# Differential attention step: one maximum instruction for both components, and the output squares taken per token tile in the next stage

## The chip, the cores and the metric

The kernel runs on one core of one Trainium2 chip. The metric is the device time of one execution in microseconds (us). The kernel before takes 1469.76 us (median of 3 runs, 1469.55 to 1470.68).

## The reference, cut to what matters

One decoder layer: an input projection; Mamba-2 and differential attention side by side; an output projection; cross-attention into 256 memory tokens; a squared-ReLU MLP. The change touches the differential attention and what follows it:

```python
def block(i):                                   # 128 queries, 4 heads, 2 components
    s = einsum('bhcqd,bhckd->bhcqk', qb, k) * scale
    s = where(causal, s, -inf)
    p = softmax(s, axis=-1)
    attn = p[:, :, 0] - lam * p[:, :, 1]
    return einsum('bhqk,bhkv->bhqv', attn, v)
o = rms_norm(o, subln_w) * (1.0 - lambda_init)  # over the 128 values of each head
```

The sequence has 1024 tokens in 8 tiles of 128. Everything is float32.

## The kernel before, in words

**The attention steps.** A step is one token tile `i` (128 queries) and one head `h`; there are 32. `ATT_STEPS` orders them in pairs of a long tile and a short one: tiles 7 and 3 for the four heads (steps 0 to 7), then tiles 6 and 2 (8 to 15), 5 and 1 (16 to 23), 4 and 0 (24 to 31). A step of tile `i` has `(i + 1) * 128` keys. The scores of a long step lie in PSUM banks 0 to 3 (two banks for each component), those of a short step in banks 4 and 5 (one for each).

Each engine has its own loop over `n`, in a fixed order written out by hand, and semaphores join them:

- TensorE: the scores of step `n` (they wait until both exponentials of step `n - 2` are done), closed by one mask matmul for each component (L2357), which signals `s_done`; then the transposes of the first four blocks of step `n - 2` (L2372), the product with the values of step `n - 3` (L2391), and the transposes of the other blocks of step `n - 2`, which use the same bank as the first four.
- VectorE: the negated maximum of component 0 of step `n` (L1643), the combination of step `n - 1` (reciprocal L1652, ratio L1653, and L1655 over all keys), the maximum of component 1 of step `n` (L1643 again).
- ScalarE: the copy of the transposed probabilities of step `n - 2` out of PSUM (L1020), the copy of the output of step `n - 3` (L1035) and its square with a sum over the 128 values (L1040), the second copy of probabilities, and the two exponentials of step `n` with their sums (L1003).

The exponential of a component waits for the maximum of that component. The transposes of a step wait for its combination.

**Extra work within the stage.** ScalarE squares the two memory tiles in its iterations 6 and 7 (L843); VectorE normalises them in iteration 9 (L1390). For each token tile, six iterations after its last head is combined or later, VectorE takes the mean of the output squares (L1374), GpSimd the power (L770), and VectorE scales the four heads (L1665).

**The end of the stage.** TensorE transposes the memory tiles in iterations 32 and 33 (L2211), ScalarE and VectorE split them in two parts each (L849, L1383), and TensorE starts the memory projections when both are split.

**The memory projection stage.** 16 steps of products with 256 columns for the memory keys and values. After every second step TensorE transposes one token tile of the mixer's output, in the order `MIX_TILES`; ScalarE evacuates each step (L1061), splits the weights (L838), and copies the transposed tile; VectorE makes the low parts.

## Time and profile before

| | |
|---|---|
| median of 3 runs | 1469.76 us |
| profiled execution, its own time | 1469.96 us |
| its span, first to last instruction | 1468.2 us |
| mean granted TensorE clock | 0.996 |
| TensorE matmul busy | 1434.4 us (98%) |
| VectorE busy | 942.7 us (64%) |
| ScalarE busy | 674.8 us (46%) |
| GpSimd busy | 89.0 us (6%) |

PE is TensorE's matmul unit and PEld its weight loads, DVE is VectorE, ACT ScalarE, POOL GpSimd. A row of the timeline gives the start and the duration in us; in square brackets stands how long the engine had been idle and what released it. "x8" means that eight records in a row are merged, and a float32 matmul of the scores and of the values product leaves two records.

### The profile page before, as it was taken

How to read it: one execution, taken by the hardware profiler on the slowest of the kernel's cores; microseconds unless marked ns; L12 is line 12 of the kernel's file. 1: busy time of each engine (PE TensorE's matmuls, PEld its weight loads, DVE VectorE, ACT ScalarE, POOL GpSimd, SP SyncE). 2: the span in 40 equal slices, each digit the busy share in tenths (PEclk: the TensorE clock that was granted, in tenths of full speed). 3: DMA queues.
4: the chain of work that ended last, by engine and by line, in shares of the span. 5: the costliest groups of instructions: out<-in, count | busy, mean ns of one | idle time of the engine just before them, and what ended most of it. 6: DMA issues, size and time to landing. Idle time of an engine off the chain costs nothing.

```text
span 1468.2 us, 19715 instructions
## 1 busy us (share of the span) xinstructions
PE 1434.4 (98%) x7272; PEld 1191.3 (81%) x7280; DVE 942.7 (64%) x1519; ACT 674.8 (46%) x1370; POOL 89.0 (6%) x132
## 2 busy tenths in 40 slices
PE   9999999998989999999999999999999999999998
PEld 8889888885669988888787877888888788888886
DVE  4883565628885434543553789887776585467897
ACT  6324222328885423432532565444454464444443
POOL 1000000000010001010000360000000000000011
PEclk9999999999999999999999999999999999999999
DMA  9212011102003612311221343664343697765463
GB/s 318 60 30 58 29 30 29 58 1 87 1 1 116 232 65 77 115 58 43 72 101 58 121 130 115 215 197 172 148 158 117 240 352 258 260 227 188 157 229 129
DMA packets 94606, 185.52 MB, mean 126 GB/s; under 512 B 10160, under 2 KB 28592, under 8 KB 92464
## 3 DMA queue, kind: packets, MB, share of 16 engines
q1 hardware_dynamic: 87312, 153.30, 30.8%
q10 hardware_dynamic: 7200, 30.97, 6.2%
q8 instruction: 58, 0.95, 0.3%
q14 instruction: 36, 0.29, 0.1%
HBM read 142.30 MB, written 41.94 MB: 125 GB/s over the span
## 4 chain that ended last, share of the span: by engine, by line
PE 87%; DVE 4%; ACT 4%; issue 3%; DMA 1%; SPq 1%; ACTq 0%; DVEq 0%; POOLq 0%; POOL 0%
PE ps L2152 26%; PE ps L2154 26%; PE ps L2153 26%; PE ps L2211 1%; ACT probs L1003 1%; DVE nmax L1643 1%; PE ps L2294 1%; DMA x_in<-in_x_dram 1%; PE ps L2391 1%; PE ps L2353 1%; PE ps L2372 1%; PE ps L2297 1%; ACT junk L843 0%; PE ps L2512 0%; PE ps L2312 0%
## 5 line engine op out<-in xcount | busy, mean ns | idle before, releaser
L2152 PE MATMUL ps<-wh,oph 128*128 128x512 f32 (+1 forms) x576 | 216.0, 375 | 0.0
L2154 PE MATMUL ps<-wh,opl 128*128 128x512 f32 (+1 forms) x576 | 212.0, 368 | 0.0
L2153 PE MATMUL ps<-wl,oph 128*128 128x512 f32 (+1 forms) x576 | 211.9, 368 | 0.0
L2152 PE MATMUL ps<-d_ring 128*128 128x512 f32 x448 | 174.6, 390 | 2.1 <-DVE d_ring L2026 2.1
L2154 PE MATMUL ps<-d_ring 128*128 128x512 f32 x448 | 174.5, 390 | 0.0
L2153 PE MATMUL ps<-d_ring 128*128 128x512 f32 x448 | 174.3, 389 | 0.0
L770 POOL TENSOR_TENSOR rms<-stat,mhalf 128x1 f32<-128x1 f32 (+2 forms) x59 | 52.6, 893 | 1329.3 <-DVE stat L1374 1307.6
L2154 PEld LDWEIGHTS ps<-wh,opl 128*128 128x128 f32 x576 | 108.3, 188 | 19.2
L2152 PEld LDWEIGHTS ps<-wh,oph 128*128 128x128 f32 x576 | 108.3, 188 | 17.8 <-ACT vt L963 0.2
L2153 PEld LDWEIGHTS ps<-wl,oph 128*128 128x128 f32 x576 | 108.4, 188 | 17.6
L1292 ACT ACTIVATE d_ring<-left_raw 128x512 fp32r<-128x512 f32 x112 | 70.3, 628 | 98.0 <-PE ps L2154 77.3
L2020 DVE TENSOR_TENSOR d_ring<-left_raw,d_ring 128x512 fp32r<-128x512 f32 x112 | 78.2, 699 | 54.8 <-ACT d_ring L1292 54.5
L2152 PE MATMUL ps<-oph,wq_h 128*128 128x512 f32 x256 | 100.8, 394 | 3.9 <-DVE wq_l L1898 2.0
L2152 PE MATMUL ps<-oph,wh 128*128 128x512 f32 x256 | 101.1, 395 | 0.7 <-DVE wl L1370 0.4
L2152 PEld LDWEIGHTS ps<-d_ring 128*128 128x128 f32 x448 | 84.1, 188 | 20.4 <-issue 2.5
L2154 PE MATMUL ps<-oph,wq_l 128*128 128x512 f32 x256 | 100.6, 393 | 0.0
L2153 PE MATMUL ps<-opl,wq_h 128*128 128x512 f32 x256 | 100.5, 393 | 0.0
L2154 PE MATMUL ps<-oph,wl 128*128 128x512 f32 x256 | 100.4, 392 | 0.0
L2153 PE MATMUL ps<-opl,wh 128*128 128x512 f32 x256 | 100.3, 392 | 0.0
L2153 PEld LDWEIGHTS ps<-d_ring 128*128 128x128 f32 x448 | 84.2, 188 | 17.4
L2154 PEld LDWEIGHTS ps<-d_ring 128*128 128x128 f32 x448 | 84.1, 188 | 17.5
L1370 DVE TENSOR_TENSOR wl<-raw,wh 128x1024 fp32r<-128x1024 f32 (+1 forms) x44 | 53.4, 1224 | 33.5 <-ACT wh L838 32.8
(358 smaller groups left out, 2938.0 us busy)
## 6 DMA issues: line engine op xcount, KB each, us to landing
right_raw<-in_w_down_dram SPq DMA_DIRECT2D x128, 256.0 KB, 3.9
u_kept_s<-us SPq DMA_DIRECT2D x64, 256.0 KB, 2.3
left_raw<-u_kept_s SPq DMA_DIRECT2D x64, 256.0 KB, 2.8
w_blk<-in_w_up_blocks_dram ACTq DMA_DIRECT2D x14, 1024.0 KB, 6.0
left_raw<-u_kept_a SPq DMA_DIRECT2D x48, 256.0 KB, 3.2
raw<-in_w_in_dram SPq DMA_DIRECT2D x16, 512.0 KB, 3.9
u_kept_a<-u SPq DMA_DIRECT2D x24, 256.0 KB, 2.3
x_in<-in_x_dram SPq DMA_DIRECT2D x8, 512.0 KB, 9.3
```

The source lines that it names most:

```text
L770: g.tensor_tensor(dst, src, mhalf[:, 0:w], ALU.pow).then_inc(rms_ready, 1)
L1003: s.activation(probs[:, n % 2, c, 0:keys], src[:, 0:keys], ACT.Exp, bias=nmax[:, n % 2, c:c + 1], accum_out=sums[:, n % 4, c:c + 1]).then_ ...
L1292: s.activation(d_ring[m % DRING][:, 0, :], left_raw[:, m % 4, :], ACT.Copy).then_inc(dn_hi, 1)
L1370: v.tensor_tensor(wl[:, slot, part], raw[:, q % 2, n], wh[:, slot, part].bitcast(F32), ALU.subtract).then_inc(w_lo, 1)
L1643: v.tensor_reduce(nmax[:, n % 2, c:c + 1], src[:, 0:keys], AX.X, ALU.max, negate=True).then_inc(mx_done[c], 1)
L2020: v.tensor_tensor(ring[:, 1, :], left_raw[:, m % 4, :], ring[:, 0, :].bitcast(F32), ALU.subtract).then_inc(dn_lo, 1)
L2152: te.matmul(o, lh, rh, start=first, stop=False)
L2153: te.matmul(o, lh, rl, start=False, stop=False)
L2154: return te.matmul(o, ll, rh, start=False, stop=last)
L2211: ins = te.transpose(ps[:, tr_bank(n) + b, k * P:(k + 1) * P], src(4 * b + k), ident[:])
L2294: te.matmul(ps[:, 4, h * 64:(h + 1) * 64], cb_decay[:, h, :], xdt[:, h * 64:(h + 1) * 64], start=True, stop=True)
L2297: ins = te.matmul(ps[:, 6, gr * 256:(gr + 1) * 256], b_cb[:, gr, :], xdt_end[:, gr * 256:(gr + 1) * 256], start=True, stop=True)
```

## The change

`s_done` and `mx_done` become one semaphore each. One `tensor_reduce` reads both components of a step and writes both maxima; it waits for both mask matmuls and stands ahead of the combination of step `n - 1`. The square with its sum is taken out of the step. In its place `o_square` squares the four heads of one token tile at a time from SBUF, and VectorE adds them up (`tensor_reduce`) ahead of the mean. Tiles 0 and 1 of `MIX_TILES` are squared in ScalarE's iterations 32 and 33 of the attention loop; tiles 2 to 7 in steps 2, 4, ... 12 of the memory projection stage. Their means are taken in the same steps and the scaling one step later.

```diff
+O_SQUARE_AT = {2 * m - 2: m for m in range(2, NT)}
+O_NORM_AT = {2 * m - 1: m for m in range(2, NT)}
...
+        o_part = [at(f"o_part{n}", "TMP", 9216 + 2048 * n, [P, DH, P]) for n in range(2)]
...
@@ ScalarE
             def attn_exp(n, c):
-                act.wait_ge(mx_done[c], n + 1)
+                act.wait_ge(mx_done, n + 1)
...
+            def o_square(m):
+                i = MIX_TILES[m]
+                act.wait_ge(o_ev, O_STEP[i] + 1)
+                if m >= 2:
+                    act.wait_ge(ms_ready, POW[("o", MIX_TILES[m - 2])] + 1)
+                else:
+                    act.wait_ge(sq_done, 2 * NT)
+                s.activation(o_part[m % 2][:], mix[:, 4:8, i * P:(i + 1) * P], ACT.Square).then_inc(o_sq, 1)
...
             for n in range(NS + 3):
+                if n in (NS, NS + 1):
+                    o_square(n - NS)
                 if n >= 3:
-                    s.activation(mix[:, 4 + h, i * P:(i + 1) * P], o, ACT.Copy, scale=recs[:, k % 4, 0:1])
-                    if k >= 4:
-                        act.wait_ge(o_ev, k - 3)
-                    elif k == 0:
-                        act.wait_ge(sq_done, 2 * NT)
-                    s.activation(junk[:, (k % 4) * P:(k % 4 + 1) * P], o, ACT.Square, scale=recs[:, k % 4, 0:1],
-                                 accum_out=stat[:, COL[("o", i)] + h:COL[("o", i)] + h + 1]).then_inc(o_ev, 1)
+                    s.activation(mix[:, 4 + h, i * P:(i + 1) * P], ps[:, 7, 0:P], ACT.Copy,
+                                 scale=recs[:, k % 4, 0:1]).then_inc(o_ev, 1)
...
             for n in range(16):
+                if n in O_SQUARE_AT:
+                    o_square(O_SQUARE_AT[n])
@@ VectorE
-            def attn_max(n, c):
-                keys = (steps[n][0] + 1) * P
-                dve.wait_ge(s_done[c], n + 1)
+            def attn_max(n):
+                i = steps[n][0]
+                dve.wait_ge(s_done, 2 * n + 2)
                 if n >= 2:
-                    dve.wait_ge(ex_done[c], n - 1)
-                b = score_bank(steps[n][0], c)
-                src = ps[:, b:b + 2, :].rearrange("p b k -> p (b k)")
-                v.tensor_reduce(nmax[:, n % 2, c:c + 1], src[:, 0:keys], AX.X, ALU.max, negate=True).then_inc(mx_done[c], 1)
+                    dve.wait_ge(ex_done[0], n - 1)
+                    dve.wait_ge(ex_done[1], n - 1)
+                b, nb = score_bank(i, 0), 2 if i >= 4 else 1
+                src = ps[:, b:b + 2 * nb, :].rearrange("p (c b) k -> p c (b k)", c=2)
+                v.tensor_reduce(nmax[:, n % 2, :], src[:, :, 0:(i + 1) * P], AX.X, ALU.max, negate=True).then_inc(mx_done, 1)
...
-            def o_mean(i):
-                dve.wait_ge(o_ev, O_STEP[i] + 1)
+            def o_mean(m):
+                i = MIX_TILES[m]
+                dve.wait_ge(o_sq, m + 1)
+                after(v.tensor_reduce(stat[:, COL[("o", i)]:COL[("o", i)] + DH], o_part[m % 2][:], AX.X, ALU.add))
                 mean(("o", i), P, DH)
...
-            for n in range(NS + 7):
+            for n in range(NS + 3):
                 if n < NS:
-                    attn_max(n, 0)
+                    attn_max(n)
                 if 1 <= n <= NS:
                     attn_comb(n - 1)
-                if n < NS:
-                    attn_max(n, 1)
...
-                if n - 7 in O_COMPLETE:
-                    o_norm(O_COMPLETE[n - 7])
-                if n - 6 in O_COMPLETE:
-                    o_mean(O_COMPLETE[n - 6])
+                if n == NS + 1:
+                    o_mean(0)
+            o_mean(1)
+            o_norm(0)
+            o_norm(1)
 
             for n in range(16):
                 for q in split_at(name, st):
                     split_lo(q)
+                if n in O_NORM_AT:
+                    o_norm(O_NORM_AT[n])
+                if n in O_SQUARE_AT:
+                    o_mean(O_SQUARE_AT[n])
@@ TensorE, scores
-                    te.matmul(..., start=False, stop=True).then_inc(s_done[c], 1)
+                    te.matmul(..., start=False, stop=True).then_inc(s_done, 1)
```

## Rows read from the trace of the kernel before

**Rows 1.** Windows: stretch, length, busy of PE, PEld, DVE, ACT, POOL, clock, DMA.

```profile
333.00:450.00 117.00, 105.26 (x746) 76.08 (x747) 93.19 (x191) 97.44 (x286) 10.96 (x14) 0.99 0.07 24
448.00:504.00 56.00, 55.87 (x461) 55.05 (x460) 31.58 (x37) 30.75 (x50) 1.30 (x2) 1.00 0.51 155
354.62:362.12 7.50, 7.50 (x54) 5.18 (x53) 6.27 (x10) 6.67 (x17) 0.00 (x0) 1.00 0.00 0
...
404.65:410.41 5.76, 5.43 (x41) 3.90 (x41) 4.76 (x12) 5.18 (x18) 1.01 (x1) 1.00 0.00 0
427.32:432.44 5.12, 4.49 (x35) 3.39 (x35) 3.94 (x12) 4.56 (x19) 1.01 (x1) 1.00 0.01 3
```

**Rows 2.** Waits from 333 to 450: us in total, times, longest.

```profile
ACT probs L1003 <- DVE nmax L1643: 10.4, 20, 1.8
```

**Rows 3.** Timeline of PE in one pair of tiles 7 and 3.

```profile
356.54 0.29 PE L2357 MATMUL ps<-mask_q,ident_b 128*128 128x128 bf16 x2
...
359.79 0.61 PE L2372 MATMUL ps<-ident,probs 128*128 128x128 f32 x4
```

**Rows 4.** Timeline of DVE in the same pair.

```profile
356.81 1.23 DVE L1643 TENSOR_REDUCE nmax<-ps 128x1 f32<-128x1024 f32 x1 [0.30 <-PE ps L2357]
357.95 0.15 DVE L1652 RECIPROCAL recs<-sums 128x2 f32<-128x2 f32 x1
...
358.40 0.75 DVE L1655 SCALAR_TENSOR_TENSOR probs<-probs,ratio 128x512 f32<-128x512 f32 x1
```

**Rows 5.** Groups by form from 333 to 450: busy us, mean ns.

```profile
L1643 DVE TENSOR_REDUCE nmax<-ps 128x1 f32<-128x1024 f32 x8 | 9.7, 1219 | 1.5 <-PE ps L2357 1.5
...
L1643 DVE TENSOR_REDUCE nmax<-ps 128x1 f32<-128x128 f32 x8 | 2.3, 282 | 0.0
...
L1655 DVE SCALAR_TENSOR_TENSOR probs<-probs,ratio 128x128 f32<-128x128 f32 x4 | 1.4, 352 | 0.1
```

**Rows 6.** The tile of the later cross-attention's maxima: ns shortest/median/longest.

```profile
L1769 DVE TENSOR_REDUCE mmax<-ps x8: 1214/1218/1225, 685.0 to 749.1; 128x4 f32<-128x1024 f32 x8
```

**Rows 7.** Timeline of PE: masks and short step's transposes, tiles 5 and 1, 4 and 0.

```profile
406.14 0.28 PE L2357 MATMUL ps<-mask_q,ident_b 128*128 128x128 bf16 x2
...
408.75 0.39 PE L2372 MATMUL ps<-ident,probs 128*128 128x128 f32 x2
...
428.60 0.28 PE L2357 MATMUL ps<-mask_q,ident_b 128*128 128x128 bf16 x2
...
430.88 0.30 PE L2372 MATMUL ps<-ident,probs 128*128 128x128 f32 x1
```

**Rows 8.** Timeline of ACT: an output square, an exponential's end, a late exponential.

```profile
355.00 0.36 ACT L1040 ACTIVATE junk<-ps,recs 128x128 f32<-128x128 f32 x1
...
355.34 0.69 ACT L1003 ACTIVATE probs<-ps,nmax 128x512 f32<-128x512 f32 x1
...
432.06 0.23 ACT L1003 ACTIVATION_READ_ACCUMULATOR probs<-ps,nmax 128x1 f32 x1
...
439.36 0.37 ACT L1003 ACTIVATE probs<-ps,nmax 128x128 f32<-128x128 f32 x1 [0.54 <-DVE nmax L1643]
```

**Rows 9.** Timeline: TensorE's two disturbed waits within the stage, and the memory tiles' normalisation.

```profile
366.74 0.63 PE L2372 MATMUL ps<-ident,probs 128*128 128x128 f32 x4 [1.29 <-ACT probs_t L1020]
...
376.57 0.55 PE L2372 MATMUL ps<-ident,probs 128*128 128x128 f32 x3 [1.18 <-DVE probs L1655]
...
372.06 2.48 DVE L1390 SCALAR_TENSOR_TENSOR h_mem<-m_in,rms,gain_b 128x1024 f32<-128x1024 f32 x2
```

**Rows 10.** Timeline of PE at the end of the stage.

```profile
439.18 0.66 PE L2372 MATMUL ps<-ident,probs 128*128 128x128 f32 x4 [1.63 <-DVE probs L1655]
...
440.85 1.91 PE L2211 MATMUL ps<-ident,h_mem 128*128 128x128 f32 x8
...
444.40 1.04 PE L2211 MATMUL ps<-ident,h_mem 128*128 128x128 f32 x8
```

**Rows 11.** Window of the slow clock there.

```profile
441.00:442.00 1.00, 1.00 (x7) 1.00 (x6) 0.00 (x0) 0.35 (x2) 0.00 (x0) 0.50 0.00 0
```

More of the change, by code:

```diff
@@ L435, in build @@
         gate_done, lam_s = sem("gate_done"), sem("lam_s")
-        s_done = [sem(f"s_done{c}") for c in range(2)]
-        mx_done = [sem(f"mx_done{c}") for c in range(2)]
+        s_done, mx_done = sem("s_done"), sem("mx_done")
         ex_done = [sem(f"ex_done{c}") for c in range(2)]
         comb_done, pt_done, pt_ev, pv_done, o_ev = (sem(n) for n in ("comb_done", "pt_done", "pt_ev", "pv_done", "o_ev"))
+        o_sq = sem("o_sq")
         resid_loaded = sem("resid_loaded")
@@ L1033, in _ @@
                     act.wait_ge(pv_done, k + 1)
-                    o = ps[:, 7, 0:P]
-                    s.activation(mix[:, 4 + h, i * P:(i + 1) * P], o, ACT.Copy, scale=recs[:, k % 4, 0:1])
-                    if k >= 4:
-                        act.wait_ge(o_ev, k - 3)
-                    elif k == 0:
-                        act.wait_ge(sq_done, 2 * NT)
-                    s.activation(junk[:, (k % 4) * P:(k % 4 + 1) * P], o, ACT.Square, scale=recs[:, k % 4, 0:1],
-                                 accum_out=stat[:, COL[("o", i)] + h:COL[("o", i)] + h + 1]).then_inc(o_ev, 1)
+                    s.activation(mix[:, 4 + h, i * P:(i + 1) * P], ps[:, 7, 0:P], ACT.Copy,
+                                 scale=recs[:, k % 4, 0:1]).then_inc(o_ev, 1)
                 if n >= 2 and n - 2 < NS and steps[n - 2][0] >= 4:
@@ L1656, in attn_comb, with o_norm @@
                                        probs[:, n % 2, 0, 0:keys], ALU.mult, ALU.add).then_inc(comb_done, 1)
-            def o_mean(i):
-                dve.wait_ge(o_ev, O_STEP[i] + 1)
+            def o_mean(m):
+                i = MIX_TILES[m]
+                dve.wait_ge(o_sq, m + 1)
+                after(v.tensor_reduce(stat[:, COL[("o", i)]:COL[("o", i)] + DH], o_part[m % 2][:], AX.X, ALU.add))
                 mean(("o", i), P, DH)
-            def o_norm(i):
+            def o_norm(m):
+                i = MIX_TILES[m]
                 dve.wait_ge(rms_ready, POW[("o", i)] + 1)
@@ L2356, in scores @@
                     kn = (i + 1) * P - (i // 4) * 512
-                    te.matmul(ps[:, score_bank(i, c) + i // 4, kn - P:kn], ident_b[:], mask_q[:], start=False, stop=True).then_inc(s_done[c], 1)
+                    te.matmul(ps[:, score_bank(i, c) + i // 4, kn - P:kn], ident_b[:], mask_q[:], start=False, stop=True).then_inc(s_done, 1)
             def mem_tile(i):
```

## The prediction, made before the changed kernel was run

> **What bounds the kernel now.** The page comes first: TensorE is busy for 98% of the span, so a change counts only where TensorE waits. The windows by stage show where that is. In the memory projections (448 to 504) TensorE is busy for 55.87 of 56.00 us, while ScalarE and VectorE have 25 and 24 us free [rows 1]. In the attention stage (333 to 450) three engines are nearly level: TensorE 105.3, ScalarE 97.4, VectorE 93.2 of 117 us [rows 1]. The pair windows split it: a pair of tiles 7 and 3 takes 7.50 us with TensorE full; a pair of 5 and 1 takes 5.76 with 5.43 busy; a pair of 4 and 0 takes 5.12 with 4.49 busy [rows 1]. The wait list then offers a bait: ScalarE waits 10.4 us for maxima, 20 times [rows 2]. But ScalarE is not full in any pair, so the question is what TensorE waits for, and this is read off the timelines. VectorE's order decides it: maximum of component 0 of the long step, combination of the short step before it, maximum of component 1 [rows 4]. TensorE takes the short step's transposes at 359.79 without a gap; the combination ended at 358.40 + 0.75 = 359.15, 0.6 us ahead [rows 3, 4].
>
> **One maximum instruction, and its place.** First the price. One component costs 282 ns for 128 keys and 1219 ns for 1024 [rows 5], so 148 ns + 134 ns per 128 keys. The cross-attention's maximum over four rows of 256 costs 1218 ns, the same as one row of 1024 [rows 6], so rows are free and 2 x (i + 1) blocks cost 0.148 + 0.268 (i + 1): 2.29, 2.02, 1.76 and 1.49 us for tiles 7, 6, 5, 4. The next instruction starts 0.09 us before the display's end (356.81 + 1.23 against 357.95) [rows 4], so a merged step saves only 0.148 - 0.09, some 0.06 us of VectorE; over 32 steps 2 us, off the path. The bounds for the saving are 0 and 0.148 a step.
>
> Then the place. The combination of the short step now stands behind both maxima of the long one. From the long step's masks to the short step's transposes TensorE has other work for 359.79 - 356.54 = 3.25 us (tiles 7, 3), 2.61 us (5, 1), 2.28 us (4, 0) [rows 3, 7]; 6 and 2 lie between, 2.93. VectorE needs from the first mask: 0.27 until the maximum starts (356.81 - 356.54), 0.05 more because the second mask counts now (two masks in 0.12 us of TensorE, my estimate), the merged maximum less 0.08, 0.45 for reciprocal and ratio (357.95 to 358.40), the combination (0.75 for 512 keys, 0.35 for 128, so 0.62 and 0.48 between) and 0.03 to wake TensorE [rows 4, 5]. Sums: 3.75, 3.35, 2.95 and 2.55. So the transposes come late by 0.50, 0.42, 0.34 and 0.27 us in each pair. TensorE is in order, and the value product of the long step and the next scores stand behind them. Late once per pair, the delay adds up, because the next maximum starts only from the next masks. In short tiles part of it was idle anyway: the next scores waited for the second exponential, whose sum ended at 432.29, 0.15 before they began at 432.44 [rows 1, 8]. That hides 0.20 in a pair of 4 and 0 and about 0.1 in the two before.
>
> **Walk through the stage**, lateness of TensorE against the trace:
> - Start: the combination of step 1 falls behind the long maximum of step 2, but ScalarE's second exponential of step 1 comes earlier. Net +0.2.
> - Steps 4 to 7 (two pairs of 7 and 3): 2 x 0.50, now +1.2.
> - Steps 6 to 9: before, TensorE stood 1.29 us for a copy by ScalarE, which was behind the two memory squares [rows 9]. There ScalarE's queue counts: it is late by 0.6 as the merged maximum releases its exponential, and gains 0.34 from the output square left out (355.00 to 355.34) [rows 8]. TensorE's lateness is absorbed in its wait: +0.3.
> - Step 10: the normalisation holds VectorE for 2.4 us [rows 9]; the combination of step 9 now stands behind it and both maxima, so its transposes come 0.7 late, of which the next scores feel 0.5: +0.5. Then two pairs of 6 and 2 at about 0.3: +1.0.
> - Tiles 5 and 1: the first pair still combines 384 keys and had waited for the transposed copy, 0; then +0.2, +0.3, and -0.1 where two of VectorE's scalings (0.6 each) are gone: +1.5.
> - Tiles 4 and 0: 0.55 - 0.27 - 0.20 = about 0.1 a pair at most: +1.6.
> - End: an exponential waited 0.54 for its maximum behind the combination [rows 8], and TensorE 1.63 for the last long combination [rows 10]. In the new order the last short maximum is out early, and two scalings and two squares are gone from the way: -0.35 for the order, -0.25 for ScalarE's squares. +1.0 at the first memory projection.
>
> **The squares.** In a step they cost ScalarE 0.34 us [rows 8], 32 times, 10.9 us. TensorE waited for ScalarE's queue only at the memory squares and at the end, which is counted above; elsewhere the exponential is released by masks, maximum and copies. In their place stand eight squares of 512 values. No row shows one; four old ones bound it at 1.44 us, one old one from below at 0.34. I take 0.6 (the 128x512 exponential is 0.69) [rows 8]. Six of them in the memory projections are 3.6 us, at most 8.6, against 25 free. VectorE gets six sums and six scalings; each is under the 1.22 us of a 1024-wide instruction [rows 5], together under 15 against 24 free [rows 1]. The chain square, sum, mean, power, scaling has one step of the stage to run in (3.3 us a step, from 16 steps and the transposes in 56 us) and the transposes want it a step later, so I cost it at nothing. If the cover failed, TensorE would wait for a scaled tile, at most about 1 us each, six times. The two squares in iterations 32 and 33 lie where ScalarE waits for TensorE's memory transposes, now that the short squares are out.
>
> **A rule against the change.** VectorE is busy for 6.27 of 7.50 us in a pair of 7 and 3 [rows 1]: not saturated. The Trainium skill (Perfetto Trace Analysis, Optimizing Scalar/DVE Operations) says that grouping into larger operations improves throughput if the engine is saturated, and that where it is not, but causes bubbles elsewhere, breaking instructions up lets work complete sooner. It puts the fixed cost of a PSUM operand on VectorE at about 125 ns: by the first half this change would give back 32 x 0.125 = 4.0 us at most, by the second half it loses. The intercept of 148 ns agrees with the figure roughly, and the idle 1.2 us say that the second half applies.
>
> **Sum.** 1469.96 (the profiled execution's own time, 1.8 above its span) + 1.0 = 1471.0; the median was 0.2 lower than that execution, so 1470.8 us.
>
> **Rivals.**
> - *Waits removed, nothing put in their place.* If the short combination still arrives in time (a cheaper merged maximum, or slack that I read too small), the gains stand alone: 0.35 at the start, 0.35 at the memory squares, 0.3 at the normalisation, 0.4 for the scalings between 410 and 417, 0.3 of waits for exponentials, 0.6 at the end: 2.3, so 1467.5; and 1466.5 if the slow clock at the end also goes. For it: the 10.4 us of waits and two engines relieved. Against it: 3.75 against 3.25 us, from measured rows.
> - *The slow clock spreads* (the other side). At 441 to 442 the clock was at 0.50, the 1.2 GHz level, after TensorE had stood for 1.63 us and a little more; eight transposes took 1.91 instead of 1.04 us [rows 10, 11], with the work after them about 1.3 us in all. It did not fall after the waits of 1.29 and 1.18 [rows 9]. The wait of step 9's transposes grows from 1.18 to about 1.65, and each pair gets a new stall of 0.3 to 0.5. It decides if any of these tips the clock: one fall gives 1472.1, two 1473.4. Against it: within pairs the new stalls are short.
> - *The late squares bite.* If the scaled tiles come late in the memory projections, up to 1 us on each of six tiles: 1472 to 1476. Against it: the 24 free us.
> - *The merge does not do what it says.* Two rows in two banks each might cost as two instructions; then +0.06 a pair more, 1471.6. It belongs to the forecast.
>
> **Chances.** Forecast 0.62, waits removed 0.20, slow clock 0.12, late squares 0.06. What a measurement of this kernel can tell from no change is about 0.2%, 2.9 us: 1466.8 to 1472.7. Of the waits-removed case under half is below that, which with a little for the unforeseen gives 0.11 for faster; slower takes most of the last two cases: 0.13; within 0.2%: 0.76. The range leaves out the tails of the rivals: 1467.4 to 1473.2 us.
>
> **What would show it.** In the profile after: 32 maxima of about 2.3 us for tile 7 and under 0.45 us for tile 0; in a pair of 7 and 3 a new wait of TensorE's short transposes for the combination (L1655 before), about 0.5 us, and a period of 8.0 instead of 7.5; ScalarE's wait for maxima of short steps gone; first memory projection about 1 us later; the stage after it unchanged in length. A period of 7.5 would prove the central step wrong, and a stage shorter by more than 1 us the whole forecast.

## The result, and the profile after

The changed kernel takes 1473.96 us (median of 21 runs, 1472.93 to 1475.95 but for one of 1590.73 at a mean granted clock of 0.85, which the ratio leaves out) against 1470.42 us (21 runs, 1468.07 to 1471.45) beside it: ratio 1.0027, interval 1.0021 to 1.0032. It is 3.5 us slower; the forecast was 1470.8 us, no change. The profiled execution took 1473.2 us, its span is 1471.5 us against 1468.2.

The forecast's central step is there. The timeline of TensorE in a pair of tiles 7 and 3, then that of VectorE (start, us busy, engine, line, operation; in brackets the idle time before it and what ended it):

```profile
356.12 1.99 PE L2371 MATMUL ps<-kt,qt 64*128 64x512 f32 x8
358.04 0.28 PE L2375 MATMUL ps<-mask_q,ident_b 128*128 128x128 bf16 x2
...
361.83 0.66 PE L2390 MATMUL ps<-ident,probs 128*128 128x128 f32 x4 [0.37 <-DVE probs L1667]
362.32 1.95 PE L2409 MATMUL ps<-vt,probs_t 128*128 128x128 f32 x16
364.20 0.70 PE L2371 MATMUL ps<-kt,qt 64*128 64x512 f32 x2
```

```profile
358.36 2.29 DVE L1655 TENSOR_REDUCE nmax<-ps 128x2 f32<-128x2048 f32 x1 [1.61 <-PE ps L2375]
360.57 0.16 DVE L1664 RECIPROCAL recs<-sums 128x2 f32<-128x2 f32 x1
360.76 0.22 DVE L1665 SCALAR_TENSOR_TENSOR ratio<-sums,recs,lam 128x1 f32<-128x1 f32 x1
361.02 0.75 DVE L1667 SCALAR_TENSOR_TENSOR probs<-probs,ratio 128x512 f32<-128x512 f32 x1
```

Before, the combination ended 0.6 us ahead of the short step's transposes [rows 3, 4]; now these wait 0.37 us for it. The pair takes 8.08 us instead of 7.50: the wait, and 0.21 us more in which TensorE is shown as busy (7.71 against 7.50; the ends of matmuls are modelled in this profile). The windows (busy time of each engine, then granted clock, DMA share, GB/s), of the memory projections and of three pairs, answer to [rows 1]:

```profile
449.00:505.00 56.00, 55.62 (x459) 54.99 (x460) 40.14 (x56) 34.25 (x56) 10.48 (x7) 1.00 0.48 148
356.12:364.20 8.08, 7.71 (x54) 5.21 (x53) 6.15 (x9) 6.66 (x15) 0.00 (x0) 1.00 0.01 2
407.22:413.39 6.17, 5.62 (x41) 3.88 (x40) 4.53 (x9) 4.56 (x13) 0.00 (x0) 1.00 0.00 0
430.52:435.77 5.25, 4.56 (x35) 3.27 (x34) 3.78 (x8) 3.92 (x13) 0.00 (x0) 1.00 0.02 5
```

What was a wait of ScalarE has become one of TensorE. The waits from 333 to 453 us (us in total, times, longest): ScalarE's 10.4 us for maxima [rows 2] are 1.7, and TensorE's for the combination were 2.8 us in 2 waits (second fence, first line) and are 5.4 us in 12.

```profile
ACT probs L1006 <- DVE nmax L1655: 1.7, 2, 1.0
```

```profile
PE ps L2372 <- DVE probs L1655: 2.8, 2, 1.6
...
PE ps L2390 <- DVE probs L1667: 5.4, 12, 1.5
PE ps L2390 <- ACT probs_t L1023: 4.0, 9, 0.8
```

At the end of the stage two rows answer to [rows 10]: the wait is 1.11 instead of 1.63 us, and the eight memory transposes take 1.05 instead of 1.91 us, as the clock is at full speed. There was no slow clock here in this execution.

```profile
442.23 0.66 PE L2390 MATMUL ps<-ident,probs 128*128 128x128 f32 x4 [1.11 <-DVE probs L1667]
...
443.80 1.05 PE L2229 MATMUL ps<-ident,h_mem 128*128 128x128 f32 x8
...
449.04 0.36 PE L2170 MATMUL ps<-memh,wh 128*128 128x256 f32 x1 [1.41 <-ACT mix L1049]
```

**Where the 3.3 us of span are,** from landmarks of the two profiles: first memory projection 447.34 to 449.04, +1.70; the residual's first transposes 561.2 to 563.2, +0.3 more; the up projection's product 4 (it waits 2.05 us for wq_l in both) 849.62 to 851.59, the same +2.0; d_ring's wait of 2.08 us 1155.47 to 1158.72, +1.28 more; from there to the end nothing (312.7 and 312.8). So 1.28 us lie almost 400 us behind the last changed instruction, in identical code. TensorE's waits there, in before and then in the changed kernel (us in total, times, longest):

```profile
PE ps L2152 <- DVE wq_l L1898: 2.0, 1, 2.0
PE ps L2152 <- DVE u_s L1952: 1.8, 1, 1.8
```

```profile
PE ps L2170 <- DVE u_s L1970: 3.2, 1, 3.2
PE ps L2170 <- DVE wq_l L1916: 2.0, 1, 2.0
```

### The profile page after: what moved, and what is told of

Same layout as the page of the kernel before. It is cut to its first block, busy times and chain, and to the rows that moved or that the text cites. A ratio compares the mean times of both kernels' runs of the same rounds, so it can differ in the third digit from the quotient of the medians.

```text
span 1471.5 us, 19613 instructions
## 1 busy us (share of the span) xinstructions
PE 1436.3 (98%) x7272; PEld 1191.1 (81%) x7280; DVE 946.5 (64%) x1495; ACT 668.2 (45%) x1314; POOL 92.3 (6%) x132
## 4 chain that ended last, share of the span: by engine, by line
PE 88%; DVE 5%; ACT 3%; issue 3%; DMA 1%; POOL 0%; POOLq 0%; DVEq 0%; ACTq 0%
PE ps L2170 26%; PE ps L2172 26%; PE ps L2171 26%; PE ps L2371 2%; PE ps L2409 1%; DMA raw<-in_w_mv_dram 1%; PE ps L2312 1%; PE ps L2229 1%; DVE wl L1381 1%; PE ps L2390 1%; DVE wq_l L1916 1%; ACT probs L1006 1%; DVE probs L1667 1%; PE ps L2237 1%; PE ps L2315 0%
## 5 line engine op out<-in xcount | busy, mean ns | idle before, releaser
L773 POOL TENSOR_TENSOR rms<-stat,mhalf 128x1 f32<-128x1 f32 (+2 forms) x59 | 56.0, 952 | 1328.9 <-DVE stat L1385 1307.5
L1381 DVE TENSOR_TENSOR wl<-raw,wh 128x1024 fp32r<-128x1024 f32 (+1 forms) x44 | 53.5, 1224 | 28.0 <-ACT wh L841 27.8
```

The costliest lines, as they stand in the source:

```text
L773: g.tensor_tensor(dst, src, mhalf[:, 0:w], ALU.pow).then_inc(rms_ready, 1)
L1381: v.tensor_tensor(wl[:, slot, part], raw[:, q % 2, n], wh[:, slot, part].bitcast(F32), ALU.subtract).then_inc(w_lo, 1)
```

## The experiments

Fifteen runs, with their own runs of before beside each group. Medians are given with them; a span or a landmark is that of the profiled execution.

**Which part costs.** Two kernels do one part alone.

`squares_only`: the squares as in the change, the maxima in two instructions around the combination, as before.

```diff
-                    attn_max(n)
+                    attn_max(n, 0)
                 if 1 <= n <= NS:
                     attn_comb(n - 1)
+                if n < NS:
+                    attn_max(n, 1)
```

> The maxima as before (one per component, the combination of the step before between them); only the squares are moved. Theory P (the place of the maximum costs): the attention stage is shorter than before by about 1.5 us: 0.3 at the memory squares, 0.4 for the scalings that leave the stage, 0.6 to 1 at the end; first memory projection at about 445.8 instead of 447.3; the memory projections give back 0.3. Total 0.5 to 1.5 us faster than before, ratio 0.9995 to 0.999. Rival S (the moved squares are what costs, in the memory projections and after them): total 1.5 us or more slower than before.

Measured: 1470.21 us (before 1469.32), ratio 1.0005 [0.9996, 1.0014]: no difference, and the expected gain of 0.5 to 1.5 us is not there. First memory projection at 444.37, 3.0 us earlier than in before's first profile, the residual's transposes only 1.1 earlier: in this profile the clock fell behind that start, at 444.6 to 448.0, and not ahead of it as in before. Against the profile of before without a fall there (before_again, below) the start is 1.2 us earlier.

`max_only`: the kernel before with the merged maximum ahead of the combination.

> Only the merged maximum ahead of the combination; the squares stay in the steps. Theory P: a new wait of TensorE's short transposes for the combination in each pair of tiles 7 and 3, 6 and 2, 5 and 1, period 8.0 to 8.1 us for 7 and 3 instead of 7.5; the first exponential 0.7 us later; first memory projection 2 to 3.5 us later than before; total 2 to 4 us slower, ratio 1.0015 to 1.0027. Rival S: within 1 us of before.

Measured: 1473.66 us (before 1469.32), ratio 1.0027 [1.0018, 1.0036], all of the loss. First projection at 448.91.

**Is it the merging or the place?**

`two_ahead`: the changed kernel with a maximum instruction for each component, both ahead of the combination.

```diff
-                v.tensor_reduce(nmax[:, n % 2, :], src[:, :, 0:(i + 1) * P], AX.X, ALU.max, negate=True)
+                for c in range(2):
+                    v.tensor_reduce(nmax[:, n % 2, c:c + 1], src[:, c, 0:(i + 1) * P], AX.X, ALU.max, negate=True)
```

> As the changed kernel, but with two maximum instructions, both ahead of the combination. If the place costs and not the merging, the pairs of 7 and 3 take 8.1 to 8.2 us as in the changed kernel (8.07) or 0.07 more, the first exponential is back at its old time (0.7 earlier), total within 1 us of the changed kernel. If the merging itself cost (a wide read of four banks, one semaphore for two masks), this is faster than the changed kernel by 1.5 us or more.

Measured: 1473.31 us, ratio 1.0024 [1.0016, 1.0033]; a pair of 7 and 3 takes 8.08 us, its wait is 0.38. In the pairs it is the place: two instructions cost the same as one. At the start of the stage it is the merging: the first exponential again starts without a wait, at 336.51, where it waits until 337.53 in the changed kernel, and step 2's scores come 1.0 us earlier (0.7 by the time from step 0's). The first projection is at 448.17, 0.9 us ahead of the changed kernel's, but the residual's transposes are not (563.27 against 563.16), and the times can't be told apart.

`short_merged`: one merged instruction in short steps alone; in long steps the combination lies between the two maxima again.

> As the changed kernel, but the long steps keep one maximum ahead of the combination and one behind it; only the short steps have the merged maximum. Theory P: TensorE's short transposes find their combination done, 7.5 us a pair of 7 and 3, the start as before or 0.3 earlier, the end 0.6 or more earlier; first memory projection at 445 to 446; total 1 to 3 us faster than before, 4 to 6 us faster than the changed kernel. Rival S: at least 1 us slower than before.

Measured: 1468.18 us, ratio 0.9991 [0.9982, 1.0000], 5.5 us below max_only and 5.1 below two_ahead, which has its squares, both run beside it. Its timelines of VectorE and TensorE in a pair of 7 and 3:

```profile
356.15 1.23 DVE L1657 TENSOR_REDUCE nmax<-ps 128x1 f32<-128x1024 f32 x1 [0.95 <-PE ps L2379]
...
357.74 0.75 DVE L1669 SCALAR_TENSOR_TENSOR probs<-probs,ratio 128x512 f32<-128x512 f32 x1
```

```profile
355.88 0.29 PE L2379 MATMUL ps<-mask_q,ident_b 128*128 128x128 bf16 x2
...
359.13 0.61 PE L2394 MATMUL ps<-ident,probs 128*128 128x128 f32 x4
```

The combination starts at 357.74, 1.86 us behind the masks at 355.88, as in before (358.40 - 356.54 [rows 3, 4]); in the changed kernel it is 361.02 - 358.04 = 2.98. The transposes have no wait, and the period is 7.5.

`max_behind`: the combination first, the merged maximum behind it.

```diff
-                if n < NS:
-                    attn_max(n)
                 if 1 <= n <= NS:
                     attn_comb(n - 1)
+                if n < NS:
+                    attn_max(n)
```

> The changed kernel with VectorE's order turned round: combination of step n-1 first, then the merged maximum of step n. Theory (the place in VectorE's queue decides, because each waits for something that the other lets happen): now the maximum can't start before the second exponential of the step before, and the chain exponential, combination, maximum, exponential, combination, maximum has nothing beside it; a pair of tiles 7 and 3 takes about 10 us instead of 8.07, a pair of 4 and 0 about 6.7 instead of 5.25, together 25 to 30 us more: about 1500 us. Rival (what costs is only that the short combination stands behind the long maximum): with the combination ahead, the short transposes are never late, the period falls back to 7.5, and the kernel comes to 1468 to 1470 us.

Measured: 1501.69 us (2 runs), 27.2 above the changed kernel run beside it (1474.45). Pairs take 10.27 us (7 and 3) and 7.82 (4 and 0; 6.7 was expected). The rows of VectorE and TensorE show the chain without anything beside it: the maximum can't start before the combination (365.29), this not before ScalarE's sum.

```profile
364.84 0.17 DVE L1664 RECIPROCAL recs<-sums 128x2 f32<-128x2 f32 x1 [1.57 <-ACT probs L1006]
...
365.29 0.75 DVE L1667 SCALAR_TENSOR_TENSOR probs<-probs,ratio 128x512 f32<-128x512 f32 x1
365.96 2.29 DVE L1655 TENSOR_REDUCE nmax<-ps 128x2 f32<-128x2048 f32 x1
```

```profile
370.72 0.70 PE L2371 MATMUL ps<-kt,qt 64*128 64x512 f32 x2 [1.21 <-ACT probs L1006]
```

**Do the squares cost anything in the memory projections?** `squares_late`: short_merged with ScalarE's square behind the rounding of the step's weights.

```diff
-                if n in O_SQUARE_AT:
-                    o_square(O_SQUARE_AT[n])
                 for q in split_at(name, st):
                     split_hi(q)
+                if n in O_SQUARE_AT:
+                    o_square(O_SQUARE_AT[n])
```

> The kernel that merges the maximum in short steps only (1468.18 us, first memory projection at 442.94, first residual transposes at 558.0), with ScalarE's squares of the outputs in the memory projections moved behind the rounding of the weights of their step. There TensorE waits 0.53 and 0.41 us for VectorE's lower halves of the weights, after ScalarE's rounding had waited for weight transfers, which start only when both halves are made. Theory (the six squares cost something because they stand ahead of the weights in ScalarE's queue, 0.6 us each, which puts off the next transfer): the waits at 483 and 497 us fall below 0.2, the residual transposes come 0.5 to 1.0 us earlier, 1467.4 us. Rival (VectorE's sums and scalings, 0.7 us each, do it, or the transfers themselves are the limit): waits and time unchanged, within 0.3 us of 1468.2.

Measured: 1468.33 us (before 1470.32), ratio 0.9983 [0.9974, 0.9992]. The wait at 483 is gone, that at 497 stays (0.47), the residual's transposes start at 557.5, 0.5 earlier. The median equals that of short_merged, so the time tells nothing. The landmark doesn't decide it either: this stretch differs by up to 1.4 us between profiles whose code in it is the same (below, under the squares).

**What repeats?** The two kernels once more.

> The kernel before, unchanged, profiled once more. In its first profile TensorE waits 1.28 us at 713 us and 1.84 us at 882 us for VectorE's u_s; in the profiles of the four changed kernels so far there is no wait at 713 and one of 3.16 to 3.18 us at 882 (the changed kernel) or the same place. Theory A: the MLP part of the loss (about 1.3 us at 882) is a property of the change; then this profile shows 1.28 and 1.84 again within 0.1. Theory B: both belong to one execution and come and go (the transfers fall differently); then this profile may show another pair of values, and the 1.3 us must not be booked to the change. Time 1469 to 1470.5 under both.

> The changed kernel, unchanged, profiled once more. Theory A: wait of 3.2 us at 884 us again, first memory projection at 449.0, first residual transposes at 563.2. Theory B: the first two numbers that lie before 600 us repeat within 0.2 us, the wait at 884 us differs. Time 1473 to 1474 under both, ratio to before 1.0025.

Measured: 1470.22 (before beside it 1470.32) and 1474.45 us. The changed kernel repeats: 448.86, 563.3, a wait of 3.17 us at 884. Before does not: its first memory projection comes at 445.54 instead of 447.34, and the wait of 1.28 us at 713 is gone (here the clock fell ahead of it, at 704.6 to 708.0, and in the first profile it did not). The wait for u_s stays (1.73). Most of the 1.80 us at the first projection is in the granted clock (the other 0.28 us were there before the wait of 1.63). Before at 440 to 444 us (clock: third column from the right), first profile, then second:

```profile
440.00:442.00 2.00, 1.45 (x8) 1.42 (x8) 0.64 (x3) 1.35 (x5) 0.00 (x0) 0.61 0.00 0
442.00:444.00 2.00, 2.00 (x12) 2.00 (x11) 0.19 (x1) 0.99 (x3) 0.00 (x0) 0.54 0.00 0
```

```profile
440.00:442.00 2.00, 1.67 (x15) 1.70 (x16) 0.40 (x2) 1.29 (x7) 0.00 (x0) 1.00 0.00 0
442.00:444.00 2.00, 1.95 (x17) 1.68 (x15) 1.29 (x2) 2.00 (x7) 0.00 (x0) 1.00 0.00 0
```

The same kernel, the same wait of 1.63 us ahead: once it went on at 1.2 GHz for 3.4 us, which is 1.7 us of full-speed time (2.00 x (0.39 + 0.46)), and once at 2.4. From the end of that wait to the first projection it took 8.16 us (439.18 to 447.34) and 6.64 (438.90 to 445.54): the fall cost 1.5 us there. And behind the wait for wq_l the clock fell in both profiles of before, and in none of the changed kernel's, which falls at 884, behind the wait of 3.2 us. The windows of before (first profile), then of the changed kernel:

```profile
850.00:852.00 2.00, 2.00 (x6) 1.53 (x5) 1.90 (x4) 0.35 (x1) 0.36 (x1) 0.51 0.00 0
852.00:854.00 2.00, 2.00 (x7) 1.61 (x6) 2.00 (x5) 1.95 (x5) 2.00 (x2) 0.64 0.00 0
...
884.00:886.00 2.00, 2.00 (x11) 1.65 (x10) 2.00 (x4) 1.97 (x5) 1.32 (x1) 1.00 0.00 0
```

```profile
852.00:854.00 2.00, 2.00 (x11) 1.63 (x10) 1.90 (x4) 0.37 (x1) 0.38 (x1) 1.00 0.00 0
...
882.00:884.00 2.00, 0.00 (x0) 0.00 (x0) 2.00 (x5) 0.04 (x1) 0.00 (x0) 1.00 0.00 0
884.00:886.00 2.00, 1.93 (x6) 1.63 (x7) 2.00 (x4) 1.97 (x4) 0.00 (x0) 0.72 0.00 0
886.00:888.00 2.00, 2.00 (x6) 1.52 (x5) 1.53 (x3) 1.97 (x5) 1.62 (x1) 0.50 0.00 0
```

This gave a second theory: between 850 and 884 VectorE's chain sets the end (it is busy without a break at 882 to 884 while TensorE does nothing). By it a slow clock ahead of that wait is hidden in it, and one behind it costs in full. Seven kernels put idle transposes of the identity into TensorE's stream to move the falls.

```diff
+                        for _ in range(14):
+                            te.transpose(ps[:, bank, 0:P], ident[:], ident[:])
```

`before_fill` (ahead of the up projection's product 0) and `before_fill_up2` (ahead of product 2), each in the kernel before:

> The kernel before with fourteen idle transposes of the identity (about 1.8 us of TensorE, their output overwritten at once) put into TensorE's wait of 2.05 us for the first lower weights of the up projection (847.9 in before). In both profiles of before the granted clock fell to 0.50 right behind that wait, TensorE's ten products from there are about 1.7 us later, and it waits 1.73 to 1.84 us at 881 to 882 for VectorE's u_s; in all changed kernels the clock stayed at 1.00 there, the wait for u_s is 3.17 us, and the clock falls behind that. Theory (VectorE's chain sets the end of this stretch, so a slow clock ahead of it costs nothing and one behind it costs 1.4 us): with the clock held up at 850 the wait for u_s grows to 3.2, the clock falls behind it, d_ring's wait starts about 1.3 us later relative to the start of the up projection, and the kernel is about 1.3 us SLOWER than before (1471.6 against 1470.3). Rival (the slow clock at 850 costs what it takes, and the 1.3 us of the changed kernels come from something else): 1.7 us faster, or no change.

> The kernel before with fourteen idle transposes (1.7 us) in front of the up projection's product 2, the one that waits 2.05 us for its lower weights and behind which the clock fell in both profiles of before. (The transposes of the run before_fill stood two products earlier, at 832 us, where VectorE's chain starts, and only delayed it.) Theory: the wait shrinks to about 0.5, the clock stays at 1.00 behind it, TensorE therefore waits 3.17 instead of 1.73 us for u_s at 880, the clock falls there, and from the start of the up projection to d_ring's wait it takes 307.2 instead of 305.9 us; the kernel is 1.3 us slower than before, unless a later fall that before shows at 1154 goes. Rival (a slow stretch costs what it takes): 1.7 us faster.

Measured: 1471.59 (before 1470.09) and 1471.61 us (before 1470.25). Both were misplaced: the wait of 2.05 us is that of product 4. It did not shrink, and the transposes delayed everything behind them by some 1.5 us, since VectorE's chain starts from TensorE's. So neither time decides anything, though both hit the expected number. The second profile still helps: this time the clock did not fall behind the same 2.05 us, and then the wait for u_s was 3.17 us and the clock fell at 884, with the code of before. Its windows:

```profile
852.00:854.00 2.00, 1.81 (x8) 1.51 (x9) 1.90 (x4) 0.00 (x0) 0.00 (x0) 1.00 0.00 0
...
884.00:886.00 2.00, 1.34 (x3) 1.11 (x4) 2.00 (x4) 1.42 (x3) 0.00 (x0) 0.68 0.00 0
886.00:888.00 2.00, 2.00 (x6) 1.58 (x5) 2.00 (x4) 1.97 (x5) 1.04 (x1) 0.50 0.00 0
```

`after_fill_up` (the changed kernel, ahead of product 13):

> The changed kernel with the same fourteen idle transposes placed in front of the up projection's product 13, the one before the wait of 3.17 us for u_s. TensorE comes to that wait 1.8 us later, VectorE does nothing else than before. Theory: wait 1.4 us instead of 3.17, the product starts at the same time, the clock does not fall behind it, and the kernel is 1.4 us faster than the changed one (1472.6 against 1474.2). Rival (the clock falls whatever fills the wait, or TensorE's lateness is handed on to VectorE): same time, or up to 1.8 us slower.

Measured: the wait is 1.57 us, the clock does not fall there, and d_ring's wait ends 305.72 us after product 4's instead of 307.13. But the clock now fell from 1157.6, behind d_ring's wait (which ended at 1157.18), where it had not in the changed kernel, and the time is 1474.55 us (6 runs), no gain. The mechanism was right, the time wrong: a fall prevented at one place came at another. The rest of the kernel took 314.1 us instead of 312.8, which gives back the 1.4. It is so in the other executions too, by their mean granted clock: the one profile with two falls (late_fill_end, the fall in the last microseconds counted) has 0.998, those with three have 0.996 or 0.997, and all six executions of after_fill_up have 0.996 or 0.997, none 0.998.

`late_fill` (squares_late, in the wait for the first cross-attention probabilities) and `late_fill_both` (ahead of product 13 as well):

> The fastest kernel so far (short steps merged, squares behind the weights; 1468.3 us) with fourteen idle transposes in TensorE's wait of 2.10 us for the first cross-attention probabilities (701 us). In seven of eight profiles of kernels with that wait the clock fell to 0.50 behind it for about 3.3 us. Theory: wait 0.3, no fall, 1.6 us faster: 1466.7. Rival (the stretch behind is set by another engine, or the clock falls a little later anyway): within 0.4 us of 1468.3.

> The kernel before this one with the transposes in front of product 13 as well. Theory: the gains add, 1.6 + 1.4: 1465.3 us, and the clock is low in the last microseconds alone. Rival: as for the two before it, 1468.3.

Measured: 1468.07 and 1468.59 us (before 1470.09). The rival holds for the first: the clock stays up, but the next probabilities are then waited for 1.40 us, and from the residual's transposes to the last of these waits it takes as long as in squares_late (557.52 to 754.06, 196.5; here 559.24 to 755.94, 196.7). A fall ahead of a wait for another engine's chain cost nothing here. The gains do not add; in late_fill_both the wait for u_s is 1.56 us, and the clock fell from 1154.2, behind d_ring's wait, as in after_fill_up.

`before_fill_end` (before, with twelve transposes in the wait of 1.63 us at the end of attention) and `late_fill_end` (the same in squares_late):

```diff
-                pe.wait_ge(comb_done, k + 1)
                 if m:
                     pe.wait_ge(pt_ev, m)
+                if (k, part) == (NS - 2, 0):
+                    for _ in range(12):
+                        te.transpose(ps[:, 6, 0:P], ident[:], ident[:])
+                pe.wait_ge(comb_done, k + 1)
```

> The kernel before with twelve idle transposes (1.3 to 1.5 us) in TensorE's wait of 1.63 us for the last long combination of attention. Of two profiles of before the clock fell behind this wait in one (first memory projection 447.34) and not in the other (445.54). Theory (before runs in two modes because this fall comes in some executions; the changed kernel's wait there is 1.11 us and its clock never fell in six profiles): no fall, first memory projection at 445.6, and a median nearer to the lower mode, 1468.5 to 1469.5 against 1470.3. Rival (the two modes of before come from elsewhere): first projection at 445.6 as well, but the same median, within 0.4 us.

> The kernel with short steps merged and squares behind the weights (1468.3 us) with the same twelve transposes in its wait of 1.41 us at 436. Behind this wait the clock fell in two of four profiles of kernels with this attention part. Theory: no fall, first memory projection at 443.0, median 0.8 us lower: 1467.5. Rival: 1468.3 unchanged.

Measured: 1468.91 us, 1.3 below before (1470.25), ratio 0.9990 [0.9981, 0.9999], just clear of none, and a range of 1468.12 to 1469.85 where before spreads from 1467.76 to 1473.11. The wait is filled and the clock holds:

```profile
437.22 1.53 PE L2372 MATMUL ps<-ident 128*128 128x128 f32 x12 [0.25 <-ACT probs_t L1020]
438.59 0.60 PE L2375 MATMUL ps<-ident,probs 128*128 128x128 f32 x4
...
440.04 1.04 PE L2211 MATMUL ps<-ident,h_mem 128*128 128x128 f32 x8
...
445.10 0.36 PE L2152 MATMUL ps<-memh,wh 128*128 128x256 f32 x1 [1.42 <-ACT junk L1040]
```

late_fill_end takes 1467.21 us, 3.0 below before, ratio 0.9983 [0.9973, 0.9993]: of all kernels the lowest median, 6.75 us below the changed one.

**The seventeen profiles together.** From product 4 to d_ring's wait the time has two values. It is 305.75 to 305.90 us in the four where the clock fell behind product 4's wait (before, before_again, before_fill, late_fill_end; wait for u_s 1.73 to 1.84), and 305.69 and 305.72 in the two with transposes ahead of product 13. It is 307.05 to 307.13 us in the other eleven: no fall there, a wait of 3.16 to 3.18 us, and a fall behind it in each. Both values occur with the code of before (305.85; 307.05, 307.06 in before_fill_up2 and before_fill_end) and with changed code (305.90 in late_fill_end; 307.13). So before's code can lose the 1.28 us too. Whether the change makes it more frequent is open: before's code gave the longer value in two of five profiles, the changed kernel and the two with its maxima (max_only, two_ahead) in all four that have no transposes there. The fall right behind the last wait for the combination came in three of the four profiles of before's attention without a filled wait, in one of five of the kernels whose short steps or squares alone are changed (late_fill, from 437.8; in squares_only and late_fill_both one came later, from 444.6 and 444.2, behind the wait of 1.41 us at the start of the memory projections), and in none of the five with the long maxima ahead of the combination. In max_behind, where that wait is 2.60 us, it came too.

## Why the prediction was wrong

**The pairs: right.** Predicted lateness of the short transposes 0.50, 0.42, 0.34 and about 0.1 us (tiles 4 and 0, after what is hidden); the periods grew by 0.58 (7.50 to 8.08), 0.36 (6.77 to 7.13 in the second profiles), 0.42 (5.76 to 6.18) and 0.13 (5.12 to 5.25). The terms hold as well: from the masks to the transposes it is 361.83 - 358.04 = 3.79 us against the 3.75 of the sum. One of them, 0.03 us to wake TensorE, stands in no row that it names; the traces have 0.06 (361.02 + 0.75 to 361.83). The merged maxima take 2292, 2023, 1758 and 1492 ns, to 10 ns as computed. two_ahead and short_merged show that the place is the cause in the pairs.

**The walk through the stage: the step that failed.** It reached +1.6 us ahead of the end. Measured at the scores of each step: +0.67 at step 2, +2.08 at step 8, +1.05 at 9, +1.20 at 10, +2.13 at 16, +3.02 at 24, +3.35 at 30. The terms that were mis-sized:
- Start, +0.2 forecast, +0.67 measured. ScalarE's first exponential now waits until both long maxima are there, and nothing stood in front of it. Before it started at 336.85 without a wait, and in two_ahead too; so this term is the merging's own. Now:

```profile
337.53 1.11 ACT L1006 ACTIVATE probs<-ps,nmax 128x1024 f32<-128x1024 f32 x1 [0.71 <-DVE nmax L1655]
```

- Steps 2 to 8: I counted two pairs at 0.50; there are three, and they cost 0.27, 0.56 and 0.58. Together with the start this is +2.08, not the +1.2 of the walk.
- The memory squares: the absorption was right, 1.03 us against 0.9. From 8 to 10 the lateness falls to +1.20 (forecast +0.5).
- Tiles 6 and 2, three pairs: 0.14, 0.36, 0.43, where I booked two at about 0.3 (0.5 + 0.6 is 1.1; the walk has +1.0). Tiles 5 and 1: 0.09, 0.35, 0.42, 0.03, where I booked 0.2 and 0.3 with a gain of 0.1 for two scalings that VectorE no longer does. Neither that gain is seen, nor the tenth of a us per pair that I took off as hidden: the full prices were 0.42 and 0.34.
- Tiles 4 and 0: 0.3 against 0.1. The end: -0.30 against -0.6, from +3.35 to +3.05 (439.18 to 442.23).

At the end of attention this is +3.05 where the walk had +1.0. Of the 2.05 us between them about 0.8 are pairs that were not booked (0.41 + 0.14 + 0.23), 0.5 the hiding that did not come, 0.5 the start and 0.3 the end. The largest fault is the count: the mechanism was priced for a pair and then booked for too few. With my own prices, hiding and all, three pairs of each kind are 3 x (0.50 + 0.3 + 0.25 + 0.1) = 3.45 us; plus 0.2 for the start, less 0.9 and 0.6, that is +2.15, and +2.8 if only the pairs of 4 and 0 hide anything.

**The clock: not in the sum.** The sum went against a profile with a fall at 440 to 444 [rows 11] and kept its 1.3 us (1.5 by the second profile) as if they belonged to the kernel. Of four profiles of before's attention one has no fall; against it the changed kernel's first projection is 3.3 us late (445.54, 448.86), not 1.7. before_fill_end supports by the time that this fall is a cost which before pays in part of its executions: without it the median is 1.3 us lower. The changed kernel has it in none of its three profiles, and its wait there is shorter. So the account of the medians, argued from the profiles and not measured, is that the change loses about 3.3 us in the stage, gets back part of the 1.5, and loses up to 1.28 behind 884 where the clock does not happen to fall at 850. Measured in all: 3.5. That the loss is in the main not a matter of the clock can be seen without profiles: beside after_again, 13 of 27 executions of before had a mean granted clock of 0.997 and took 1470.1 us on average, and seven of the changed kernel's eleven had the same clock and took 1473.5.

**The slow clock as a rival: its place was wrong.** I priced more falls inside attention; in the changed kernel there is none. What differed is the wait at 884, 3.2 us instead of 1.8 with a fall behind it, that no row of mine covered, since I took everything behind the stage as shifted rigidly.

**The squares: nearly right.** Costed at nothing in the memory projections. From the first memory projection to the residual's transposes it takes 113.9 us in both profiles of before, and 114.1 to 114.5 in the changed kernel's three. But the four other profiles without the squares there take longer too: 114.3 in before_fill_end, 114.6 in max_only, 114.8 and 115.3 in before_fill_up2 and before_fill, with waits for weights of up to 0.9 us in all. The mean of all six is 114.5 us; that of the six with the squares ahead of the weights and no fall in the stretch (the changed kernel's three, two_ahead, short_merged, max_behind) is 114.6. A small cost can't be told from that spread. In attention the squares alone bring 1.2 us (squares_only, against the profile of before without the fall), and its time shows no gain. short_merged, which keeps the place of the long combination, starts the memory projections 2.6 us earlier by the same comparison (445.54, 442.94), where the rival *waits removed* counted 2.3. Its median is 1.1 us below before's beside it, with an interval that reaches 1.0000; squares_late, with the same attention, is 2.0 below, clear of noise. So the rival was right on what there was to gain and wrong that this order lets it through.

**The rule against the change** pointed the right way: VectorE was not saturated, and longer instructions made a bubble on TensorE. That the 148 ns of a start could be saved played no part: two_ahead, which pays it, is not slower than the change (1473.31, against 1473.66 of max_only beside it). The merging had a price of its own instead, once: the first exponential, 0.7 us.

**Open.** What decides whether the clock falls behind a given wait. Behind 3.2 us it fell eleven times of eleven, behind product 4's 2.05 us four times of seventeen, behind d_ring's 2.08 three of seventeen, and behind the 2.1 us for the first cross-attention probabilities thirteen of the fifteen times that it was not filled, with the same code ahead. So the length of the wait alone doesn't decide it. Open too is whether the change makes the longer way past 884 more frequent.

## What to carry to other kernels

An instruction merged out of two is worth its start-up time, and costs as much as its second half delays whatever stood between the two, and whoever could have started on the first half alone: before merging, look at who stood between, and at the slack of its consumer. Price such a delay per repetition and multiply by all repetitions; a walk that stops to absorb here and there loses count. Before summing against one profile, look for clock falls in it, and for each ask which engine's chain ends behind it: one hidden by a wait was free here, and it may vanish and reappear behind that wait in another kernel or another execution of the same one. The mean granted clock of the executions that were not profiled is a cheap second look.

## What the runs showed of the hardware

- In these seventeen profiles the granted clock falls to half in stretches of about 3.4 us. One cost 1.5 us at the end of attention (8.16 against 6.64), 1.4 behind d_ring's wait (314.1 against 312.8 to the end), and nothing ahead of a wait for another engine. Whether one comes differs between executions of one kernel: 1.63 us of idle TensorE at the end of attention was followed by it in the first profile of before and not in the second.
- VectorE's sums of 128x512 with both inputs in SBUF, 0.68 us elsewhere, take up to 1.8 us while GpSimd works on tiles of that size; those with one input in PSUM keep 0.68 us. In that profile 19 with both inputs in SBUF ran for the most part beside such a GpSimd instruction: 12 took 0.80 to 1.80 us, 7 kept 0.68. The 12 all began 0.2 to 1.1 us behind the start of a GpSimd instruction and ended 0.55 us behind its end; of the 7, six began with it or ahead of it. Of 17 with an input in PSUM none took more than 0.70. Ten of the 12 lie between 856 and 882, in VectorE's chain ahead of the wait at 884; what they add to that wait was not measured. From the second profile of the changed kernel, VectorE and GpSimd:

```profile
856.02 1.80 DVE L1916 TENSOR_TENSOR wq_l<-w_blk,wq_h 128x512 fp32r<-128x512 f32 x1
857.75 0.68 DVE L1970 TENSOR_TENSOR u_s<-ps,p_s 128x512 f32<-128x512 f32 x1
```

```profile
855.43 1.84 POOL L783 TENSOR_TENSOR t_sum<-raw_t,t_sum 128x512 f32<-128x512 f32 x1
```

The Trainium skill (SBUF — State Buffer, Who interferes with whom) says that a VectorE instruction with two SBUF inputs contends with a GpSimd instruction that reads SBUF, as they share a port, and one with at most one such input, outside the two-port modes, does not. The trace agrees, with 1.80 and 0.68 in the rows above; the seven of the 19 that kept 0.68 show that not every overlap costs.
- GpSimd's power of 4 columns takes 1.0 or 2.0 us in the memory projections, though nothing about its operands changes from one tile to the next. What changes is what VectorE had begun. In the eleven profiles with these powers, six in each behind the first, 19 began while VectorE's low part of the weights (L1381, both inputs in SBUF, 1.23 us) was running or with it: all took 1.91 to 2.09 us. The other 47, where it began later or not at all, took 1.01. The rows of the changed kernel, GpSimd then VectorE, a long power and a short one:

```profile
460.14 2.08 POOL L773 TENSOR_TENSOR rms<-stat,mhalf 128x4 f32<-128x4 f32 x1 [9.04 <-DVE stat L1385]
...
479.96 1.01 POOL L773 TENSOR_TENSOR rms<-stat,mhalf 128x4 f32<-128x4 f32 x1 [4.40 <-DVE stat L1385]
```

```profile
460.13 1.23 DVE L1381 TENSOR_TENSOR wl<-raw,wh 128x1024 fp32r<-128x1024 f32 x1
...
480.28 1.23 DVE L1381 TENSOR_TENSOR wl<-raw,wh 128x1024 fp32r<-128x1024 f32 x1 [0.40 <-ACT wh L841]
```
